# The second half's input projection inside the first half's lead: two matmuls behind each tick of heads and transposes, one behind each tick of attention

## What is computed

```python
def trunk(x, c, ...):
    cond = silu(c)
    for l in range(2):
        sh_m, sc_m, g_m, sh_f, sc_f, g_f = split(cond @ ada_w[l] + ada_b[l])     # 6 x 1024
        h = rms_norm(x, norm_mix_g[l]) * (1 + sc_m) + sh_m
        if l == 0:
            proj = h @ w_in_ab               # 1024 x 1952: the projection of this change
            q_lat, kv_lat, k_pe, bq, bk, bv = split(proj)
            y = (latent attention, differential attention, head norm) @ w_out_ab
        else:
            y = chunked_attention(h @ w_in_c) @ w_out_c
        x = x + g_m * y
        h = rms_norm(x, norm_ffn_g[l]) * (1 + sc_f) + sh_f
        x = x + g_f * peer_ffn(h)            # 128 picks of a token, one row of 2048 floats each
```

## Time and profile before

| | us |
|---|---|
| median of 3 runs | 3324.57 |
| the profiled execution | 3332.64 |
| its span, first to last instruction | 3330.7 |
| heads, 9 ticks (127.2 to 145.9) | 18.7 |
| transposes, 25 ticks (145.9 to 177.1) | 31.2 |
| attention, plain ticks (177.1 to 206.2) | 29.1 |
| attention, differential ticks (206.2 to 271.2) | 65.0 |
| last ticks of attention up to the next part (271.2 to 278.8) | 7.6 |
| first gather | 370.3 |

### The profile page before, as it was taken

The page is one execution under the profiler, slowest core; times in us unless marked ns, Lnnn a source line. Parts: engine busy times, 40 slices in busy tenths (PEclk is TensorE's granted clock), DMA queues, the critical chain, the costliest instruction groups (busy, mean ns, idle before and its releaser), DMA issues. The chain is left out here.

```text
span 3330.7 us, 29036 instructions
## 1 busy us (share of the span) xinstructions
PE 2658.0 (80%) x8188; PEld 1476.4 (44%) x8188; DVE 2424.1 (73%) x5581; ACT 1185.6 (36%) x3370; POOL 1233.4 (37%) x1085
## 2 busy tenths in 40 slices
PE   5798788768868888788768888788868899777776
PEld 4575544334445443365445444365445444322322
DVE  7775788788877788756976888746967878754544
ACT  1141233358822333313822333314842223323222
POOL 0110245344444445333334444434333345433332
PEclk9899899988788999888778999988768999999999
DMA  8782799999999999999999999999999999999997
GB/s 320 271 288 92 276 420 409 364 360 346 351 381 414 384 421 412 418 386 369 377 374 418 395 421 414 413 376 366 375 357 379 412 402 412 417 422 404 421 421 324
DMA packets 266714, 1247.23 MB, mean 374 GB/s; under 512 B 20117, under 2 KB 106533, under 8 KB 135351
## 3 DMA queue, kind: packets, MB, share of 16 engines
q0 software_dynamic: 156064, 1106.97, 82.2%
q1 hardware_dynamic: 110482, 138.36, 11.6%
q10 hardware_dynamic: 8, 0.06, 0.0%
HBM read 1243.18 MB, written 7.36 MB: 375 GB/s over the span
## 5 line engine op out<-in xcount | busy, mean ns | idle before, releaser
L1554 PE MATMUL psum<-space 128*128 128x512 f32 x3192 | 1618.2, 646 | 411.3 <-ACT space L1598 365.6
L1688 POOL DMA_INDIRECT space<-in_peer_uv,expert x1024 | 1200.6, 1172 | 1833.2 <-PE psum L1554 1170.3
L1629 DVE CUSTOM_DVE_ANT_0 space<-space,h 128x1024 f32<-128x1024 f32 x1024 | 1246.6, 1222 | 655.3 <-DMA space<-in_peer_uv,expert 630.2
L1554 PEld LDWEIGHTS psum<-space 128*128 128x128 f32 x3192 | 618.3, 203 | 1166.0 <-issue 573.9
L1587 ACT ACTIVATE space<-space 128x2 f32<-128x2 f32 x512 | 103.9, 203 | 1492.8 <-DVE space L1629 1482.3
L713 PE MATMUL psum<-space 128*128 128x256 f32 (+2 forms) x1584 | 388.0, 403 | 69.8 <-DMA space<-in_w_in_c 33.1
L713 PEld LDWEIGHTS psum<-space 128*128 128x128 f32 x1584 | 315.2, 202 | 161.2 <-issue 55.0
L1598 ACT ACTIVATE space<-ident,space 128x128 f32<-128x128 f32 x798 | 278.1, 387 | 1.7 <-PE psum L1554 0.2
L1231 PE MATMUL psum<-space 128*128 128x256 f32 x1024 | 263.1, 386 | 13.8 <-DVEq L574 5.3
L1231 PEld LDWEIGHTS psum<-space 128*128 128x128 f32 x1024 | 198.7, 195 | 139.5 <-issue 105.5
L1590 ACT ACTIVATE space<-space,gate 128x1 f32<-128x1 f32 x1024 | 245.6, 287 | 16.8
(11 more groups left out here) (181 smaller groups left out, 1821.9 us busy)
## 6 DMA issues: line engine op xcount, KB each, us to landing
space<-in_peer_w_q SPq DMA_DIRECT2D x32, 1024.0 KB
space<-in_ada_w SPq DMA_DIRECT2D x12, 2048.0 KB, 15.7
space<-in_ada_w POOLq DMA_DIRECT2D x24, 1024.0 KB, 5.6
space<-in_w_in_c SPq DMA_DIRECT2D x24, 1024.0 KB
space<-in_peer_uv,expert POOLq DMA_INDIRECT x1024
space<-in_w_out_ab SPq DMA_DIRECT2D x8, 1024.0 KB
space<-skewed SPq DMA_DIRECT2D x32, 256.0 KB
space<-in_w_out_c SPq DMA_DIRECT2D x8, 1024.0 KB
```

Source lines behind the costliest of these rows:

```text
L1554: last = nc.tensor.matmul(b.bank[part][:, :], b.diag2[:, n % DIAGS, :], b.pairs[:, p % PAIRS, 1, part * BANK:(part + 1) * BANK], start=(p ...
L1629: dve.tensor_tensor_reduce(out=row, in0=row, in1=b.h[:, tile(q), :], scale=1.0, scalar=0.0, op0=ALU.mult, op1=ALU.add, accum_out=b.dots2[: ...
L1688: pool.indirect_dma_start(out=b.pair_rows[q % PAIRS], out_offset=None, in_=ins["peer_uv"], in_offset=bass.IndirectOffsetOnAxis(ap=b.expert ...
```

## The change

The projection starts at tick 29 instead of tick 50. `project` yields after every matmul, and a list says how many steps are taken behind each tick: 2 behind heads and transposes, 1 behind attention. That is 18 matmuls in heads, 50 in transposes and 52 in attention; the last 8 follow at tick 114. Before it was two matmuls behind each of ticks 50 to 113: 26 in transposes, 102 in attention. ScalarE's emptying follows the same list. GpSimd's order of loads becomes S0 W0 S1 W1, S2 S3 S4, W2, S5 S6, W3, S7 S8, W4, S9 S10, W5, S11 S12 S13, W6, S14 to S17, W7, S18 to S23. Nothing is added to or taken from what is computed.

```diff
-AHEAD = 2
+AHEAD = 1
...
-        normed, projected, latents, headed, attended, head_normed, put_out = (
-            ticks_in(lead[:n]) for n in (1, 2, 3, 4, 6, 7, 9))
-        between = headed + 12
+        normed, projected, latents, headed, turned, attended, head_normed, put_out = (
+            ticks_in(lead[:n]) for n in (1, 2, 3, 4, 5, 6, 7, 9))
+        ahead_steps = [0] * latents + [2] * (headed - latents) + [2] * (turned - headed) + [1] * (attended - turned)
...
-                if between < taken < attended:
+                for _ in range(ahead_steps[taken - 1] if taken <= attended else 0):
                     next(project, None)
...
-                if between < taken < attended:
+                for _ in range(ahead_steps[taken - 1] if taken <= attended else 0):
                     next(empty, None)
...
-            for n in range(2, ahead.n_chunks):
-                for i in range(loaded, 2 * n + 7):
+            for n, upto in zip(range(2, ahead.n_chunks), (5, 7, 9, 11, 14, 18)):
+                for i in range(loaded, upto):
                     second.load(pool, i)
-                loaded = 2 * n + 7
+                loaded = upto
                 ahead.load(pool, n)
```

## The result

The changed kernel takes 3367.6 us (median of four runs, 3353.7 to 3371.9) against 3327.2 us of the kernel before (four runs): a ratio of 1.0115, 95% interval 1.0079 to 1.0151. It is 40 us slower; 8 us faster was forecast.

What follows compares the result with a forecast made beforehand. TensorE was taken to bound the differential ticks, S loads the plain ones. Terms -13.8 + 3.4 + 1.0 + 0.7 + 0.6 = -8.1 us took the median from 3324.6 to 3316.5 us; 8-in-10 range 3308 to 3327.

Steps and rivals of the forecast that it cites:

- Differential ticks, -13.8 us: 32 differential attention ticks each lose one 0.43 us matmul; tick 1.61 us, TensorE still the bound: -13.8 us.
- The clock as a rival: Transposes: TensorE at 1.2 GHz after idling, all 25 ticks 54 us, 23 more; 3338.8 us, chance 0.03.
- Plain ticks, +1.0 us: Plain attention ticks: S loads decide, S14 waits behind W6, first differential scores start later: +1.0 us.
- W7 and S18, +3.4 us: Differential ticks: S18 queued behind W7 lands late, VectorE stands about 5 us, costing TensorE 3.4 us; bounds 0 and 5.
- Transposes and heads, +0.7 us: Transposes: added matmuls hidden, W loads delay S loads, +0.7 us, bounds 0 and 5.7; heads: 18 matmuls, 0.
- End of attention, +0.6: Last ticks: three matmuls less in them, nine at the very end, then a copy: +0.6 us.
- Carried over one to one: Behind the lead: gathers unchanged, so the lead's gain or loss shifts the whole rest to the end by as much.
- VectorE as bound: Differential ticks: VectorE's waits persist, tick 1.83 us, only 6.5 us gained; sum -0.8 us, 3323.8 us; chance 0.15.
- Loads starve: Transposes: S loads behind W loads land 11.4 us after issue, 5.8 us more each; 3339 us, chance 0.08.
- The loads fall clear: Attention: W6 and W7 issued early enough that VectorE's stalls never reach TensorE; -13.2 us, 3311.4 us, chance 0.27.

Runs made afterwards that it cites:

- e_best: Changed kernel with S14 issued before W6, S18 before W7, and the bias-row copy issued after the lead's output weights: 3314.1 us, ratio 0.9951.
- b_stall: Kernel before with 14 useless VectorE additions, about 10 us, at tick 79, the first differential one: 3388.8 us, ratio 1.0172.
- e_order: Changed kernel with only S14 issued before W6 and S18 before W7: ten runs, 3309.0 to 3377.5 us, ratio 0.9987 without the three longest.
- e_fill: Changed kernel with zero matmuls added behind nearly every projection matmul in ticks 75 to 114: four runs, 3342.3, 3377.0, 3386.6 and 3409.7 us.
- e_best2: e_best with its attention projection in groups of four matmuls behind every fourth tick: 3326.3 us, ratio 0.9993.
- b_stall_burst: b_stall with four projection matmuls behind every second tick instead of two behind each: 3336.7 us, ratio 1.0023 against the kernel before.

## Why the prediction was wrong

- **Differential ticks, -13.8 us: the step that failed.** "TensorE stays the bound" was right, and the length of the tick too: 1.60 us in e_best against 1.61. Wrong was that it would run at full clock. With the clock at 1.2 GHz the tick measured 2.94 us, +28.9 us for the stretch. I had priced an idle gap at its own length, 3.4 us; its real price was every tick behind it. That a gap of this size drops the clock is shown by b_stall (a gap alone, put into the kernel before) and by e_best (no gap, no fall).
- **The clock as a rival** was on record, with a chance of 0.03, and for the wrong place. In the transposes the clock was up for most of the time, as argued (0.93, low from about 147.3 to 150.7 and behind the last). What could have warned me stood in the earlier trace rows: there TensorE, released after a long idle time, ran projection matmuls at the low clock for several ticks. I took that as a matter of the transposes. The question to ask was what happens behind each gap that my own sum puts into attention. TensorE was busy without a break for 94 us in the changed kernel, and for 113 us in b_stall, and its clock stayed at 1.2 GHz. The Trainium skill, "TensorE: Matmul & The Clock Gate", Part 1, says that "the default state is throttled, and activity releases the throttle"; in these two stretches the measurement differs, and decides. What the Trainium skill says in Part 4 of that page, that transposes don't count as busy in the same way, no run here shows by itself: the same transposes stood in the plain ticks, where the clock came back, and in the differential ones, where it didn't.
- **Plain ticks, +1.0 us: mechanism right, size wrong.** W6 in front of S14 was named, with a stand of VectorE of about 5 us. Measured were 7.0 us, and +4.9 us up to the first differential scores. S14 was issued 22.4 us after the start of attention, not 19.3: TensorE reached the end of tick 74, for which W6 waits, late, since S12 had come late (VectorE waited 3.6 us, TensorE 2.11) and the clock was low from 195.0 to 198.4. S14 then took 10.7 us to land.
- **W7 and S18, +3.4 us:** VectorE stood 3.7 us at S18 where I had put 5, at slow ticks. At the low clock it cost TensorE nothing.
- **Transposes and heads, +0.7 us:** +1.9 measured, of which heads 0.5 (the first transposes start at 146.7 instead of 146.2); within the bounds of 0 and 5.7. TensorE was busy for 16.2 us in heads, where I had 16.6. **End of attention, +0.6:** +2.6 measured, the same matmuls at a clock of 0.80.
- **Carried over one to one:** roughly. The profiled execution of the changed kernel is 34.9 us longer with a first gather 40.3 later, that of e_best 14.5 us shorter with one 18.3 earlier.
- **The other rivals.** VectorE as bound: refuted by e_best, where VectorE keeps up with ticks of 1.60 us. Loads starve: its mechanism took part, as the trigger, but its price of 5.8 us a load was not what made the kernel slow. The loads fall clear: it took e_best, with order and copy changed, to make that case true, and there the sum holds: 65.0 - 51.2 = 13.8 us for the differential ticks, the term of the sum, 4.0 for the plain ones within the bound of 4.4, and 2.5 in the last ticks, less 1.3 for a later start: the part after attention starts 19.0 us earlier.

What stays open: when exactly a short gap drops the clock. In e_order it fell behind one of 1.41 us (2.17 and 0.19 us had gone before), in e_fill it did not behind one of 2.37 us. What in a plain tick brings the clock back, and is missing in a differential one, was not tested apart. And why the clock fell without any gap in e_best2 was not separated further than that three ticks without projection stood between the groups.

## What to carry to other kernels

Price an idle gap of TensorE not by its length but by the clock behind it: look for the stretch that follows, and ask what in it could bring the clock back; here most groups of four projection matmuls did, and so did the plain ticks, with scores on 96 rows, but the differential ticks, with scores on 32, did not. A fall cost an estimated 1.7 us in the one (half of 3.4 us at the low clock in the changed kernel) and 29 us in the other. A tick of mixed small work can hold a high clock that it can't regain. So before work is moved out of such a stretch, clear it of stalls first, above all of a load that waits for its own engine in front of one that doesn't (one queue, in order): with the order changed and the copy out of the way the same change went from +1.1% to -0.5%.

## What the runs showed of the hardware

- The granted clock has a memory of this kind: the same differential ticks ran 51 us at 2.4 GHz without falling (e_best) and 94 us at 1.2 GHz without rising (after), each time with TensorE busy 100% of the time. These two differ in the order of the loads and the place of the copy as well; b_stall differs from the kernel before in a stall alone, and its ticks took 3.79 instead of 2.04 us for the rest of the 32.
- The same fall was made good in the plain ticks: the clock was low from 195.0 to 198.4 in the changed kernel, 196.0 to 199.4 in e_order and 194.0 to 197.4 in e_fill, with TensorE busy throughout.
- After a gap of 6.6 us two projection matmuls behind each tick left it low for 113 us; the same matmuls in groups of four, after a gap of 7.6 us, had it back at the end of the first group (b_stall and b_stall_burst).
- Ten runs of one kernel (e_order) fell into two heaps about 50 us apart. A single time of such a kernel can lie in either.
